# RWKV stage: two of eight chunks of the projections and gating columns as three split products

## What is computed

```python
z = h @ w_in                       # columns [gMLP u, v | RWKV r, k, v | low-rank parts]
z = z + (_token_shift(z) - z) * mu # RWKV columns alone
r, k, v, xw, xa, xg = jnp.split(z, ...)
a = jax.nn.sigmoid(a0 + xa @ a2)
kk = hv(k * k_k); kk = kk / jnp.maximum(jnp.sqrt(jnp.sum(kk * kk, -1, keepdims=True)), 1e-12)
k = k * (1 + (a - 1) * k_a)
y = _wkv7_scan(r, decay, k, v, -kk, kk * a)   # per head and token: state*w + sa*b + v*k
u, vg = gelu(zu), gelu(zv)                    # the gating columns, used in the next stage
```

## Time and profile before

| | |
|---|---|
| three runs, median (lowest to highest) | 2926.93 us (2925.25 to 2927.55) |
| the profiled execution, its own time | 2926.73 us |
| its span, first to last instruction | 2925.0 us |
| stage of the pairs | 1499.0 to 2043.7 us of the span |
| mean granted TensorE clock | 0.986 of full |

### The profile page before, as it was taken

The page is one execution under the profiler, slowest core; times in us unless marked ns, Lnnn a source line. Parts: engine busy times, 40 slices in busy tenths (PEclk is TensorE's granted clock), DMA queues, the critical chain, the costliest instruction groups (busy, mean ns, idle before and its releaser), DMA issues. The chain is left out here.

```text
span 2925.0 us, 48206 instructions
## 1 busy us (share of the span) xinstructions
PE 2796.2 (96%) x19709; PEld 2170.2 (74%) x19709; DVE 1756.6 (60%) x2526; ACT 1271.4 (43%) x2051; POOL 562.4 (19%) x383
## 2 busy tenths in 40 slices
PE   8999999999999999999999989998799999999997
PEld 6877767777777777777756576678678788888884
DVE  2332163685566666666425354353885899999995
ACT  2111020222454554453323222232443788888883
POOL 2222132222322222213231010101000111111102
PEclk9999999999999999999999999999799999999999
DMA  5111211754222221113221020113663799999997
GB/s 176 40 40 47 86 66 58 216 190 129 59 58 58 59 58 53 56 47 120 73 71 41 24 69 23 62 62 129 199 230 153 299 395 395 401 393 390 397 388 285
DMA packets 232144, 445.60 MB, mean 152 GB/s; under 512 B 18256, under 2 KB 160096, under 8 KB 206608
## 3 DMA queue, kind: packets, MB, share of 16 engines
q1 hardware_dynamic: 224896, 426.07, 41.0%
q0 software_dynamic: 7056, 16.79, 1.6%
HBM read 389.78 MB, written 61.94 MB: 154 GB/s over the span
## 5 line engine op out<-in xcount | busy, mean ns | idle before, releaser
L1223 DVE TENSOR_TENSOR fox_pT_lo<-psum,fox_pT_hi 128x512 fp32r<-128x512 f32 (+2 forms) x192 | 107.0, 557 | 179.3 <-ACT fox_pT_hi L1162 169.9
L1030 PE MATMUL psum<-x_hi,w_hi 128*128 128x512 f32 x512 | 210.8, 412 | 2.3 <-PEq L100 1.7
L1032 PE MATMUL psum<-x_hi,w_lo 128*128 128x512 f32 x512 | 200.9, 392 | 0.0
L1031 PE MATMUL psum<-x_lo,w_hi 128*128 128x512 f32 x512 | 200.2, 391 | 0.0
L3162 POOL DMA_INDIRECT xg<-n_rows,idx x33 | 84.1, 2549 | 476.7 <-PE psum L3049 454.9
L1733 PE MATMUL psum<-hT,wr 128*128 128x512 f32 x384 | 167.1, 593 | 0.0
L3272 DVE TENSOR_TENSOR lo_g<-land_g,hi_g 128x2048 fp32r<-128x2048 f32 x68 | 152.8, 2288 | 16.8 <-ACT hi_g L3198 16.8
L1173 ACT ACTIVATE fox_p<-fox_p,fox_bias 128x256 f32<-128x256 f32 (+7 forms) x128 | 99.6, 778 | 118.2 <-DVE fox_bias L1209 114.8
L3272 DVE TENSOR_TENSOR lo_u<-land_u,hi_u 128x2048 fp32r<-128x2048 f32 x66 | 150.4, 2282 | 0.0
L3272 DVE TENSOR_TENSOR lo_d<-land_d,hi_d 128x2048 fp32r<-128x2048 f32 x64 | 143.5, 2283 | 0.0
L181 PE MATMUL psum<-x_hi,w_hi 128*128 128x512 f32 x352 | 138.4, 393 | 0.0
(11 more groups left out here) (564 smaller groups left out, 7325.2 us busy)
## 6 DMA issues: line engine op xcount, KB each, us to landing
land_g<-in_moe_w_gate SPq DMA_DIRECT2D x66, 1024.0 KB, 7.5
land_u<-in_moe_w_up SPq DMA_DIRECT2D x66, 1024.0 KB, 7.5
land_d<-in_moe_w_down SPq DMA_DIRECT2D x64, 1024.0 KB, 8.2
ada<-in_ada_w SPq DMA_DIRECT2D x24, 1024.0 KB
y_slots<-yb SPq DMA_DIRECT2D x33, 512.0 KB, 9.4
w<-in_w_in SPq DMA_DIRECT2D x27, 512.0 KB, 6.5
wo<-in_w_out SPq DMA_DIRECT2D x12, 1024.0 KB, 9.9
w_land<-in_w_kv_shared SPq DMA_DIRECT2D x23, 512.0 KB, 4.1
```

Source lines behind the costliest of these rows:

```text
L1030: nc.tensor.matmul(bank[:], hi[:, d, :], E.x_hi[:, d, cols], start=(d == 0), stop=False)
L1031: nc.tensor.matmul(bank[:], hi[:, d, :], E.x_lo[:, d, cols], start=False, stop=False)
L1032: last = nc.tensor.matmul(bank[:], lo[:, d, :], E.x_hi[:, d, cols], start=False, stop=(d == ND - 1))
```

## The change

- The last two of the eight chunks of h (`IN_THREE`) enter the projections and the fills as three split products each; the first six stay whole. The low-rank columns stay whole.
- hi and lo are made in this stage. For h once: ACT copies two chunks into `h_hi`, DVE subtracts in place (`h_lo` lies on those chunks of `E.hT`), after the low-rank products have read them. For each weight: ACT rounds 128x256 to `w_hi` one projection ahead, DVE subtracts in place (`w_lo`). For each block of gating columns the same with 128x512 (`uv_hi`, `uv_lo`): the first in the step of r, the others at the end of `turn` (ACT) and the start of `A` (DVE).
- Two weight buffers instead of three: SP loads number m + 2 when the last half of m is complete.
- New semaphores tell of each part. PE waits for them after the six whole chunks: for the weight at the first half of each projection, for h in the first projection, for the gating block in its first fill.
- `v` lies in the third weight buffer's place, `rate` in a place that was free; `w_hi` and `uv_hi` lie where the low-rank weight was. `ws` is loaded after one more wait, for the last pair's bonus products, which read `rate`.

The diff, without most of the placing of buffers:

```diff
+IN_THREE = (ND - 2, ND - 1)
-        NW = 3
-        w = [E.sb(f"wr_{i}", [P, ND, P], ctx=st) for i in range(NW)]
+        NW = 2
+        split = slice(IN_THREE[0], ND)
...
@@ PE, proj
-                        bank = take(ringD, (kind, c, hf))
-                        for d in range(ND):
-                            last = nc.tensor.matmul(bank[:], w[m % NW][:, d, :], E.hT[:, d, hf * HALF:(hf + 1) * HALF],
-                                                    start=(d == 0), stop=(d == ND - 1))
+                        bank, cols = take(ringD, (kind, c, hf)), slice(hf * HALF, (hf + 1) * HALF)
+                        for d in range(IN_THREE[0]):
+                            nc.tensor.matmul(bank[:], w[m % NW][:, d, :], E.hT[:, d, cols], start=(d == 0), stop=False)
+                        if hf == 0:
+                            pe.wait_ge(S_["w_lo"], m + 1)
+                        if m == 0:
+                            pe.wait_ge(S_["h_lo"], len(IN_THREE) * (hf + 1))
+                        for i, d in enumerate(IN_THREE):
+                            hi, lo = E.w_hi[m % NW][:, i, :], w_lo[m % NW][:, i, :]
+                            nc.tensor.matmul(bank[:], hi, h_hi[i][:, cols], start=False, stop=False)
+                            nc.tensor.matmul(bank[:], hi, E.h_lo[:, i, cols], start=False, stop=False)
+                            last = nc.tensor.matmul(bank[:], lo, h_hi[i][:, cols], start=False, stop=(d == ND - 1))
@@ PE, fill
+                        for d in range(IN_THREE[0]):
+                            nc.tensor.matmul(bank[:, 0:UVW], E.hT[:, d, rows], w_uv[:, d, :], start=(d == 0), stop=False)
+                        if t == 0:
+                            pe.wait_ge(S_["u_lo"], q + 1)
+                        for i, d in enumerate(IN_THREE):
+                            u_hi, u_lo = E.uv_hi[:, i, :], uv_lo[:, i, :]
+                            nc.tensor.matmul(bank[:, 0:UVW], h_hi[i][:, rows], u_hi, start=False, stop=False)
+                            nc.tensor.matmul(bank[:, 0:UVW], h_hi[i][:, rows], u_lo, start=False, stop=False)
+                            last = nc.tensor.matmul(bank[:, 0:UVW], E.h_lo[:, i, rows], u_hi, start=False, stop=(d == ND - 1))
@@ SP, ahead
+                        sp.wait_ge(ringA.full, ringA.nth(("bonus", NPAIR - 1)))
@@ ACT
+                def weight_highs(m):
+                    act.wait_ge(w_landed[m % NW], 16 * (m // NW + 1))
+                    nc.scalar.copy(E.w_hi[m % NW][:], w[m % NW][:, split, :]).then_inc(S_["w_hi"], 1)
+                def uv_highs(q):
+                    act.wait_ge(uv_landed, 16 * (q + 1))
+                    nc.scalar.copy(E.uv_hi[:], w_uv[:, split, :]).then_inc(S_["u_hi"], 1)
                 def lora():
+                    for i, d in enumerate(IN_THREE):
+                        nc.scalar.copy(h_hi[i][:], E.hT[:, d, :]).then_inc(S_["h_hi"], 1)
...
+                    weight_highs(0)
                     act.wait_ge(ringD.free, ringD.nth(("lora", 0, 1)))
                 def proj(c, kind):
+                    m = 3 * c + KIND.index(kind)
+                    if m + 1 < 3 * NPAIR:
+                        weight_highs(m + 1)
+                    if m == 0:
+                        uv_highs(0)
@@ ACT, turn, at its end
+                    if c > 0:
+                        uv_highs(c)
@@ DVE
+                def weight_rests(m):
+                    dve.wait_ge(S_["w_hi"], m + 1)
+                    part = w[m % NW][:, split, :]
+                    nc.vector.tensor_tensor(w_lo[m % NW][:], part, E.w_hi[m % NW][:].bitcast(F32), ALU.subtract).then_inc(S_["w_lo"], 1)
...
                 def lora():
                     for i, (n, to) in enumerate(((2 * LORA, xwa), (GATE_LORA, E.xg))):
+                        if i == 1:
+                            dve.wait_ge(ringD.full, ringD.nth(("lora", 1, 1)))
+                            h_rests(0)
+                            weight_rests(0)
+                            h_rests(1)
                 def proj(c, kind):
+                    if 3 * c + i + 1 < 3 * NPAIR:
+                        weight_rests(3 * c + i + 1)
+                    if c == 0 and i == 0:
+                        uv_rests(0)
                 def a_part(c):
                     if c > 0:
+                        uv_rests(c)
```

More of the change, by code:

```diff
@@ L1606, in gains @@
             link(dve, V.scalar_tensor_tensor(m, m, 1.0, self.gain[:, i * ND:(i + 1) * ND], ALU.add, ALU.mult))
+IN_THREE = (ND - 2, ND - 1)
 def stage_rwkv_pairs(nc, E, A):
     with ExitStack() as st:
-        NW = 3
-        w = [E.sb(f"wr_{i}", [P, ND, P], ctx=st) for i in range(NW)]
+        NW = 2
+        split = slice(IN_THREE[0], ND)
+        w, w_lo = [], []
+        for i in range(NW):
+            with ExitStack() as raw:
+                w.append(E.sb(f"wr_{i}", [P, ND, P], ctx=raw))
+            E.sb(f"wr_place{i}", [P, ND - len(IN_THREE), P], ctx=st)
+            w_lo.append(E.sb(f"wr_lo{i}", [P, len(IN_THREE), P], F32R, ctx=st))
         w_landed = [E.sem(f"wr_landed{i}") for i in range(NW)]
+        v = E.sb("v", [P, S], ctx=st)
         wl = E.w_lora
@@ L1638, in stage_rwkv_pairs @@
         restart = E.sb("restart", [P, S], ctx=st)
-        E.sb("z_place", [P, 1 + S], ctx=st)
+        rate = E.sb("rate", [P, 1 + S], ctx=st)[:, 0:S]
         lw, cl, e2, tmp = (E.sb(x, [P, S], ctx=st) for x in ("lw", "cl", "e2", "tmp"))
@@ L1648, in stage_rwkv_pairs @@
         r = [E.sb(f"r{i}", [P, S], ctx=st) for i in range(2)]
-        k, v, at, bt, rate = (E.sb(x, [P, S], ctx=st) for x in ("k", "v", "at", "bt", "rate"))
+        k = E.sb("k", [P, S], ctx=st)
+        h_hi = [E.sb("h_hi0", [P, S], F32R, ctx=st)]
+        at, bt = (E.sb(x, [P, S], ctx=st) for x in ("at", "bt"))
+        h_hi.append(E.sb("h_hi1", [P, S], F32R, ctx=st))
         ctr = E.sb("ctr", [P, NC], ctx=st)
@@ L1660, in stage_rwkv_pairs @@
         ringD = Ring(E.banks[4:8], E.sem("rwD_full"), E.sem("rwD_free"))
-        w_uv = E.sb("w_uv", [P, ND, UVW], ctx=st)
+        with ExitStack() as raw:
+            w_uv = E.sb("w_uv", [P, ND, UVW], ctx=raw)
+        E.sb("w_uv_place", [P, ND - len(IN_THREE), UVW], ctx=st)
+        uv_lo = E.sb("uv_lo", [P, len(IN_THREE), UVW], F32R, ctx=st)
         uv_rows = [E.sb(f"uv_rows{i}", [P, UVW], ctx=st) for i in range(2)]
@@ L1667, in stage_rwkv_pairs @@
         uv_landed, uv_stored = E.sem("w_uv_landed"), [E.sem(f"uv_stored{i}") for i in range(2)]
-        S_ = {x: E.sem("rw_" + x) for x in ("rest", "kept", "sq", "cc", "front", "level", "exp1", "exp2", "exp3", "stored", "tanh", "rstore", "ab")}
+        S_ = {x: E.sem("rw_" + x) for x in ("rest", "kept", "sq", "cc", "front", "level", "exp1", "exp2", "exp3", "stored", "tanh", "rstore", "ab", "h_hi", "h_lo", "w_hi", "w_lo", "u_hi", "u_lo")}
         w_in = A["w_in_2"][0].rearrange("(c p) n -> p c n", p=P)
@@ L1779, in fill_ @@
                             pe.wait_ge(uv_landed, 16 * (q + 1))
[L1780 to L1783, removed]
+                        bank, rows = take(ringA, ("uv", q, t)), slice(t * P, (t + 1) * P)
+                        for d in range(IN_THREE[0]):
[7 more added lines that the diff above has]
+                            last = nc.tensor.matmul(bank[:, 0:UVW], E.h_lo[:, i, rows], u_hi, start=False, stop=(d == ND - 1))
                         last.then_inc(ringA.full, 1)
@@ L3638, in build_program @@
             modulated = ExitStack()
-            E.xT = far("hT", modulated)
+            with ExitStack() as raw:
+                E.xT = far("hT", raw)
+            E.h_lo = E.sb("h_lo", [P, len(IN_THREE), S], F32R, ctx=modulated, side="right")
+            E.sb("hT_rest", [P, ND - len(IN_THREE), S], ctx=modulated, side="right")
             E.run(stage_out, A, 1, x1_rows, x2_rows, modulate=True, whole=2)
@@ L3642, in build_program @@
         with ExitStack() as second:
-            E.sb("w_lora_kept", [P, ND, 2 * LORA + GATE_LORA], ctx=second)
+            E.w_hi = [E.sb(f"wr_hi{i}", [P, len(IN_THREE), P], F32R, ctx=second) for i in range(2)]
+            E.uv_hi = E.sb("uv_hi", [P, len(IN_THREE), UVW], F32R, ctx=second)
+            E.sb("w_lora_rest", [P, ND * (2 * LORA + GATE_LORA) - len(IN_THREE) * (2 * P + UVW)], ctx=second)
             E.bonus = E.sb("bonus", [P, NT, 2 * NPAIR], ctx=second)
```

9 lines of the change are left out of this document (added).

## The result

The kernel after takes 2902.47 us (median of 3 runs, 2900.66 to 2904.32) where the kernel before took 2926.93: a ratio of 0.9915, 95% interval 0.9899 to 0.9931. The profiled execution took 2900.66 us; its page begins, as in the earlier trace rows, with

What follows compares the result with a forecast made beforehand. PE's own stream was taken to bound the stage of the pairs. 8.2 + 2.0 + 4.6 + 2.1 - 1.9 - 0.4 = 14.6 us off 2926.73 gave 2912.1 us; forecast range 2907 to 2915 (chance 0.60), wider range 2905.5 to 2920.5.

Steps and rivals of the forecast that it cites:

- Projections, 8.2 us: 48 chunk products in the projections, each three split passes at 0.23 us instead of two whole ones: 0.17 us gained each.
- the tails behind them, 2.0 us: Time from a projection's last weight load to the next step's: 0.20 us shorter at ten projections followed by small products.
- Fills, 4.6 us: 64 chunk products of 256 gating columns, 0.425 us whole and 0.353 split at a pace of 0.118: 0.072 us gained each.
- their tails, 2.1 us: Time behind the last load of 22 fills followed by small tiles: 0.09 us gained each, assumed between nothing and 0.20.
- the slower rival: Narrow split products in the fills run at the wide ones' pace, costing 17 us at 0.23: 2934 us; chance 0.05.
- Swallowed, 2.3 us: Gain lost where PE waits on other engines: 1.9 us at eight fills, 0.4 us at the first round's turn of v.
- Preparation, places, nothing: About 9 us more rounding on ACT and 11 us more subtracting on DVE stay hidden; moving v and rate costs nothing.
- Two buffers, nothing: Later weight loads and ACT's new waits for their landing cost nothing; 0.6 us to spare at the tightest place.
- a sign to look for: Among the signs of a right forecast: no ACT idle time in the stage ended by the landing of a weight.
- Instruction refills: PE's holes of about 2.35 us at instruction packet boundaries: taken as zero, two holes either way for the range.
- holes that vanish: Case of a time better than 2907 us because refill holes on PE disappear; chance 0.03.
- half again as fast: Refill rival: split products use up instructions that fast, four to six more holes, 2921.5 to 2926 us; chance 0.11 with landings.

Runs made afterwards that it cites:

- whole products in both: Kernel after with whole products again in projections and fills, waits keeping every instruction packet's end in place: ratio 0.9943 to the kernel before, stage 526.4 us.
- the kernel before with waits only: Kernel before plus waits that compute nothing ahead of each sum's last two chunk products, giving the kernel after's packet ends: ratio 0.9959, stage 527.4 us.
- the shifts: Either kernel with 64, 128 or 192 idle waits added early in the stage (phases; 0 is unshifted): ratios 0.9937 to 1 before, 0.9915 to 0.9982 after.

## Why the prediction was wrong

- **Projections, 8.2 us, and the tails behind them, 2.0 us.** The pace (0.23, no hole at the switch) was right. Right too is the 0.55 us at the end; wrong is to add it. With the boundaries kept, all projections together go from 167.5 us (whole products in both) to 159.5 (after): 8.0, tails included. The earlier trace rows showed the other half of the tail, the first split load at the old pace; the forecast quoted it and counted 0.17 us for that product all the same.
- **Fills, 4.6 us, and their tails, 2.1 us.** Pace 0.118 as forecast from the earlier trace rows, so the slower rival is out. Measured step by step, the fills give 3.6 us with the tails in them, where these two terms had 6.7 (22 x 0.09 is 2.0 and not 2.1). A fill between small tiles gains 0.15 us and not 0.144 + 0.09, the same double count (18 fills, 1.4 us); the rest are the four behind X, which the forecast took off under "swallowed", and those ahead of a projection, which give 0.06.
- **Swallowed, 2.3 us.** The four fills behind X give nothing, as forecast: they last 4.05 to 4.19 us with whole products and 4.07 to 4.12 with split ones. That is in the 3.6 us already. 8.0 + 3.6 are 11.6 us and 9.4 arrive, so 2.3 us (unrounded) go elsewhere, but not where the forecast had them: an estimated 1.7 us are the fallen clock at 1963, and PE's waits for ACT and DVE grow by 0.9 us (12.9 to 13.8). In the three later rounds PE waits 1.3 us each for DVE (at) in the turn (first row of the waits after), a place that the forecast did not name. But so does the kernel before with waits only (3.9 us there too), where no product is faster: the wait takes back a part of the vanished holes.
- **Preparation, places, nothing.** Right: -1.0 us. ACT and DVE got 7.7 and 9.2 us more work (forecast 9 and 11).
- **Two buffers, nothing.** Right as a price, wrong as a sign to look for: ACT's idle time is ended three times by a weight's landing.

```profile
ACT wr_hi L2086 <- DMA wr<-in_w_in: 6.4, 3, 3.5
```

  PE pays nothing for it: its waits for ACT are 7.2 us in this kernel and in the kernel before with waits only.
- **Instruction refills: "I take zero, and two holes either way".** This is the step that failed. That a boundary moved can give as well as cost was right, and the hole's price was read rightly from the earlier trace rows. The size was off: the term, put at zero, measured 13.7 us in the stage (12.0 by the ratio, 7.6 to 16.4). Its parts, from the kernel before to that with waits only, come to 13.4 us: 14.7 us of issue waits less, 5.5 us of waits for ACT and DVE more, since those chains had been hidden in the holes, and 4.2 us of PE's busy time less, which the forecast's price of a hole lacked (below). The forecast allowed this term 4.7 us either way; four phases of the same kernel span 10.6 us before and 15.1 us after. The case "holes that vanish" had been given 0.03. (Among the rivals, "half again as fast" is too low: six instructions in 0.69 us against four in 0.86 are 1.9 times as fast.) As the shifts now show, the 24.5 us of issue waits before stood near the top of what the kernels here have (9.0 to 25.4), so a gain was likelier than a loss; the sum of all rows of PE's issue waits, of which the forecast read single ones, is the number that could have raised the question.
- **Sum.** Of the forecast's 14.6 us the two tail terms, 4.1, hold what the paces had already given; at equal packet ends the change is worth 9.4 us in the stage (10.3 from the kernel before with waits only). The mean over the shifts 0, 64, 128 and 192 is 536.2 us before and 525.7 after, 10.5 apart. Of the 24.5 us measured, about half (13.7 by the stage, 12.0 by the ratio) is where the packets happen to end: luck, not the change's own merit.

## What to carry to other kernels

A change that adds or removes instructions on the busiest engine also shifts every packet end behind it, and in a stream with dense levels of small products that alone was worth 18 to 20 us of 2927 here: before a small gain is believed, compare at equal packet ends (waits that cost nothing make up the count) or over several shifts. What a step saves is read from the whole step, from its first weight load to the first load of the next; a pace and a tail added up hold the same time twice where the pace changes inside the step. And where holes go, look at which chains they had covered: here 15 us of holes less were 9 us net of the waits that came up in their place, and 4 us of PE's busy time on top, 3.4 of it clock.

## What the runs showed of the hardware

Behind a hole the clock may go as well. Stretches of the kernel before around the hole of 2.87 us at 1700.08 (PE busy, PEld, DVE, ACT, POOL, then the granted clock, DMA share, GB/s):

```profile
1697.00:1700.00 3.00, 3.00 (x138) 3.00 (x138) 2.96 (x5) 1.12 (x2) 0.00 (x0) 1.00 0.95 298
1700.00:1703.00 3.00, 0.41 (x23) 0.27 (x13) 1.74 (x2) 0.06 (x1) 0.00 (x0) 1.00 0.27 84
1703.00:1705.00 2.00, 2.00 (x16) 1.93 (x16) 0.69 (x1) 1.05 (x2) 0.00 (x0) 0.74 0.10 37
1705.00:1708.00 3.00, 3.00 (x19) 3.00 (x18) 0.00 (x0) 2.13 (x5) 0.00 (x0) 0.60 0.95 384
1708.00:1710.50 2.50, 2.50 (x42) 2.48 (x44) 0.00 (x0) 1.48 (x4) 0.00 (x0) 1.00 0.98 309
```

The granted clock goes from full (2.4 GHz) to means of 0.74 and 0.60, that is to 1.2 GHz for much of the 5 us behind the hole, and the turn of k takes twice as long as that of v (eight loads in 1.72 and 0.90 us):

```profile
1703.20 0.90 PEld L1765 LDWEIGHTS psum<-ident,v 128*128 128x128 f32 x8
1704.08 1.72 PEld L1765 LDWEIGHTS psum<-ident,k 128*128 128x128 f32 x8
```

The same turns in the kernel after with whole products in both, where PE stood for 1.55 us and not for 2.73:

```profile
1697.00:1699.00 2.00, 0.69 (x7) 0.45 (x6) 1.97 (x3) 1.07 (x2) 0.00 (x0) 1.00 0.00 0
1699.00:1703.50 4.50, 4.50 (x48) 4.48 (x52) 1.04 (x2) 3.07 (x7) 0.00 (x0) 1.00 0.58 232
```

Behind the hole at 1665.5 (2.4 us) of the kernel before the clock fell too, and behind that of the earlier trace rows (2.35 us) it stayed full:

```profile
1668.00:1671.50 3.50, 3.45 (x35) 1.63 (x37) 1.28 (x2) 1.76 (x3) 0.00 (x0) 0.76 0.02 5
1671.50:1674.00 2.50, 2.50 (x62) 2.50 (x62) 2.17 (x2) 2.29 (x4) 0.00 (x0) 0.65 0.02 7
1752.80:1756.00 3.20, 3.20 (x26) 2.82 (x27) 1.28 (x2) 0.00 (x0) 0.00 (x0) 1.00 0.02 5
```

So PE's busy time isn't independent of its standing. By these rows an estimated 1.7 us of full clock are missing behind each of the two holes (2.00 x 0.26 + 3.00 x 0.40, and 3.50 x 0.24 + 2.50 x 0.35), 3.4 us in all, and the kernel with waits only has no such stretch. That explains 3.4 of the 4.2 us of busy time that went with the holes; the rest is open. What tells a hole that costs clock from one that doesn't isn't shown here.
